# Moving a weight load, dummy products and a few rows of work in a fused two-block transformer kernel

## The chip, the cores and the metric

The kernel runs as one program on one core of one Trainium2 chip. The metric is the device time of one execution in microseconds (us). Before the change the median of 3 runs is 746.59 us (744.43 to 747.97).

## The reference

Two transformer blocks are computed on one sequence of 256 tokens with 1024 features, all in float32. The first block is an attention and pooling mixer followed by a mixture of 32 experts; the second is a hybrid mixer (attention and a recurrence) with a feed-forward layer.

```python
mod = jnp.matmul(c_act, w_ada[l]) + b_ada[l]
sh_m, sc_m, gt_m, sh_f, sc_f, gt_f = jnp.split(mod, N_MOD, axis=-1)
...
x = x + gt_m[:, None, :] * mix
h = modulate(rmsnorm(x, norm_ffn_g[l]), sh_f, sc_f)
ffn = hierarchical_moe(h.reshape(B * S, D), ...)
x = x + gt_f[:, None, :] * ffn.reshape(B, S, D)
...
for g in range(N_EXPERT_GROUPS):
    a = jnp.einsum('td,edf->tef', h, w_gate[g])
    b = jnp.einsum('td,edf->tef', h, w_up[g])
    act = jax.nn.silu(a) * b * comb[:, g, :, None]
    y = y + jnp.einsum('tef,efd->td', act, w_down[g])
...
xn = rmsnorm_2(x, norm1_g[layer])
u = xn @ w_in[layer].astype(f32)
```

`gt_f`, the gate row of the experts' output, is columns 5120 to 6143 of `mod`. The second block begins with the product of the normed result and its own `w_in`.

## The kernel before

**Pieces and their queue.** All large weights come from memory in 194 pieces of 1 MB (128 x 2048 float32), in the order of a list `pieces`: 36 for the first mixer, then the expert pieces from `E0` = 36 to `E1` - 1 = 131, then the second block's, whose first is piece `E1` (`w_in_2`). All are issued from SyncE (SP) by `sp_piece`, one after the other; `slot[i]` says into which of 25 places of SBUF piece i goes, and SP waits until the piece that was there before has been freed by the engine that read it. The list `ends` gives the places of the last 18 expert pieces. The places `HL` and `HL + 1` (raw15 and raw16 in the profile) share their memory with `XB`, the high and low parts of the normed input; `XP` is the memory of `X`, `XR` is `rawx`.

**Experts.** The 32 experts are worked off in 8 rounds y of 4 experts. A round has 8 pieces of gate and up weights (`pe_gate_up`, two halves of 4 pieces) and 4 pieces of down weights (`pe_down`, n = 0, 1 for the output half, f = 0, 1 for the piece). TensorE (PE) multiplies each piece in four strips of 32 rows (`psum<-raw,G` and `psum<-raw,XT`, 8 instructions a piece). Between them ScalarE (ACT) and VectorE (DVE) compute silu and product, PE turns the result (`pe_act`), DVE multiplies by the gate row (`dve_results`) and PE adds the result to the tokens in PSUM banks 4 to 7 (`pe_combine`, `psum<-ym,WT`). Ahead of round 7 every engine runs through the test of an overflow flag (a branch).

**Into the experts.** `dve_products` sums `w_ada` pieces weighted by `c` into `acc`; `pe_gate_row` then forms the gate row of half b by a product of ones with `acc`, plus a product with one row of ones for the bias `GTF`. In `pe_mixer`, `pe_mix_part`(n) is followed by `pe_back`(n - 1), which needs the DVE's row `x1`(n - 1) (L974). DVE works out the router (`dve_route`), up to the mask `MK`; PE ranks it (`psum<-MK,...`), DVE makes places and a selection `SS`, and PE gathers the tokens (`psum<-SS,XNH`). The first free place for the next expert piece comes when PE has multiplied the first one (`psum<-X,G`).

**Into the second block.** A piece of `w_in_2` is split by ACT into a high part (`whi`, L492) and by DVE into the rest (`wlo`, L503). `pe_n3` turns the experts' result, ACT and DVE make `XB` of it (`dve_n3`, L2163), and `feature_part` multiplies in groups of three matmuls (`psum<-XB,whi` twice, `psum<-XB,wlo` once).

**PSUM banks.** There are 8. `Banks(ids).take(e, name)` hands them out in the order of its list and lets the engine wait until the bank's last result has been read. The second block takes its banks from one such list nearly to its attention part, where `pe_z` has its own list `zb` = [0, 1, 2]. `pe_awake` is a dummy product, 128 x 512, whose result nobody reads.

Of the kernel before, what the change touches and what calls it, by code (L numbers as in the profile page):

```python
# [105 lines left out]
def build(nc, a, out):  # L106
# [3 lines left out]
    with root:  # L110
# [240 lines left out]
        for i in range(NP):  # L351
            if i == E0:
                last = homes[-NR - 1:]
                parts_ = [NR + k + NS * h for k in range(NS) for h in range(2)]
                turns = [XP] + last[0:5] + parts_[0:2] + last[5:] + parts_[2:] + [HL, HL + 1]
                first = turns[0:2] + [GP] + turns[2:12] + [YP] + turns[12:]
                ends = [NR, NR + NS] + parts_[2:6] + [(E1 + k) % NR for k in range(NR)] + parts_[6:] + [HL, HL + 1, XP]
            if pieces[i][0] == "exp":
                n = i - E0 - len(first)
                k = first[n] if n < 0 else turns[n % len(turns)] if i < E1 - len(ends) else ends[i - E1 + len(ends)]  # L360
                last_exp[k] = i
            elif i in fixed:
# [83 lines left out]
        def sp_load(e, upto):  # L446
            while cur["sp"] < min(upto, NP):
                i = cur["sp"]
                cur["sp"] += 1
                if i != E0:  # L450
                    sp_piece(e, i)
# [63 lines left out]
        def dve_products(e, b, k):  # L515
            s, i = acc[b % 2], ai[(b, k)]
            r = ring[slot[i]]
            e.wait_ge(*landed(i))
            for c in range(4):
# [84 lines left out]
        def pe_gate_row(e, banks, b):  # L604

            p = banks.take(e, ("ada", b))
            e.wait_ge(*loaded("gtf"))
            mm(e, p[:, :], ones[0:1, :], GTF[0:1, 512 * (b % 2):512 * (b % 2) + 512], True, False)
            e.wait_ge(*at(("acc", b)))
            mm(e, p[:, :], ones[:, :], acc[b % 2][:, :], False, True).then_inc(*moe_pe(("ada_sum", b), ("accread", b)))  # L610
# [56 lines left out]
        def feature_part(e, banks, j, cs, name, xname="n1", steps_=None):  # L667
            steps_ = steps_ or mix_pe
            h, l = whi[j % NS], wlo[j % NS]
            for q in range(2):  # L670
# [189 lines left out]
        def dve_mixer(e):  # L860
# [109 lines left out]
            dve_products(e, 11, 1)  # L970
            for n in range(8):
                e.wait_ge(*at(("mix_sum", n)))
# [317 lines left out]
        def pool_moe(e):  # L1290
            for n in X1:
                e.wait_ge(*at(n))
            overflow(e, "pool", None, None)
# [176 lines left out]
        def pe_moe(e, banks):  # L1470
# [3 lines left out]
            pe_awake(e, p, 2)  # L1474
# [11 lines left out]
            for y in range(NQ + 1):  # L1486
# [29 lines left out]
                if y < NQ:  # L1516
                    pe_gate_up(e, p, y, 1)
# [3 lines left out]
                if y and y != NQ - 1:  # L1521
                    for n in range(2):
                        pe_down(e, db, y - 1, n)
                        if y == NQ:
                            if n:
                                pe_n3(e, Banks([1]), 0)
                                pe_n3(e, Banks([3]), 1)
                            pe_combine(e, y - 1, n)
# [7 lines left out]
        def pe_down(e, db, y, n):  # L1536
            b = y % 2
            e.wait_ge(*at(("a", y)))
            p = db.take(e, ("d", y, n))
            for f in range(2):  # L1540
# [38 lines left out]
        def pe_gate_up(e, p, y, half):  # L1579
            g = y // 2  # L1580
            for c in range(4 * half, 4 * half + 4):
# [7 lines left out]
                x.then_inc(*moe_pe(("freed", i), *[("gu", y)] if c == 7 else []))  # L1589
            return p  # L1590
# [176 lines left out]
        def act_hybrid(e):  # L1767
            e.preload_act_table_set("natural_log_exp_and_others")
            for t in range(2):
                act_square(e, t, 0)  # L1770
            for q in range(4):
                if q == 2:
                    for t in range(2):
                        act_square(e, t, 1)
                high_part(e, E1 + q // 2, q % 2)
# [5 lines left out]
            act_pieces(e, E1 + 4)  # L1781
            for t in range(2):
# [169 lines left out]
        def dve_hybrid(e):  # L1952
# [3 lines left out]
            dve_results(e, NQ - 1, (1,))  # L1956
            low_part(e, E1, lo_dve, 0)
            dve_n3(e, 0)
            for t in range(2):
                dve_xg(e, t, 1)  # L1960
            low_part(e, E1, lo_dve, 1)
            dve_n3(e, 1)
            dve_n3(e, 2)
            low_part(e, E1 + 1, lo_dve, 0)
# [242 lines left out]
        def pe_hybrid(e, banks):  # L2207

            zb, ob, sb_, wb = Banks([0, 1, 2]), Banks([3, 4, 5, 6, 7]), Banks([2, 0, 1, 3]), Banks([4, 5, 6, 7])
            fb = Banks([0, 2])  # L2210
            feature_part(e, fb, w2(0), (0, 1), "f", "n3", hyb_pe)
            pe_n3(e, Banks([4]), 2)
            pe_n3(e, Banks([5]), 3)
            feature_part(e, fb, w2(0), (2, 3), "f", "n3", hyb_pe)
# [362 lines left out]
        def tensor_engine(e):  # L2577
            pe_mixer(e)
            pe_moe(e, Banks(list(range(8))))
            banks = Banks([6, 7, 0, 1, 2, 3, 4, 5])  # L2580
# [84 lines left out]
```

## Time and profile before

| | |
|---|---|
| median of 3 runs | 746.59 us |
| profiled execution, its own time | 746.17 us |
| span in its trace | 743.1 us |
| PE busy | 683.2 us (92%) |
| DVE busy | 390.0 us (52%) |
| ACT busy | 290.4 us (39%) |
| mean granted clock of TensorE | 0.963 |
| read from memory | 206.20 MB |

Times below are microseconds from the span's start. A granted clock of 1.00 is TensorE's full 2.4 GHz, 0.50 the lower level, 1.2 GHz. The chain that ended last is 67% PE and 19% DMA. A profile's "x" counts instructions; a float32 product is two of them.

### The profile page before, as it was taken

What the parts mean: (1) busy time and instruction counts of PE and PEld (TensorE: products, weight loads), DVE (VectorE), ACT (ScalarE), POOL (GpSimd) and SP (SyncE); (2) the same over time, 40 slices, a digit from 0 to 9 for tenths busy, and PEclk for the clock granted to TensorE, in tenths of its full rate; (3) what the DMA queues carried; (4) which work ended last, traced back from release to release, by engine and by line L of the source; (5) the groups of instructions that cost most, each with busy time, mean ns of one, the idle gap of its engine ahead of it and who ended that gap; (6) DMA issues with size and microseconds to landing.
All of it is one profiled execution on the core that took longest, in us unless ns stands there. A gap on an engine that the chain in (4) does not pass through costs nothing.

```text
span 743.1 us, 12343 instructions
## 1 busy us (share of the span) xinstructions
PE 683.2 (92%) x5124; PEld 514.0 (69%) x5124; DVE 390.0 (52%) x617; ACT 290.4 (39%) x425; POOL 53.9 (7%) x96
## 2 busy tenths in 40 slices
PE   4999998999978677777999999999999999999996
PEld 3897888653423121223999989998988888888885
DVE  3677776332110100104867987655876765665653
ACT  4245430241111010004676552578366544344532
POOL 0010000000000000000048650000000000000000
PEclk9999999799998798889999999999999999999998
DMA  9999999989999999999944534411654545664001
GB/s 369 426 423 417 387 392 415 427 343 424 427 427 426 426 427 427 424 426 427 365 191 160 209 120 161 171 58 62 228 210 158 217 144 206 227 227 168 3 1 56
DMA packets 29568, 208.10 MB, mean 280 GB/s; under 512 B 3266, under 2 KB 3522, under 8 KB 4676
## 3 DMA queue, kind: packets, MB, share of 16 engines
q1 hardware_dynamic: 29508, 207.26, 69.1%
q8 instruction: 43, 0.70, 0.4%
q14 instruction: 17, 0.14, 0.0%
HBM read 206.20 MB, written 1.05 MB: 279 GB/s over the span
## 4 chain that ended last, share of the span: by engine, by line
PE 67%; DMA 19%; DVE 6%; ACT 4%; issue 3%; SPq 1%; DVEq 0%; ACTq 0%
PE psum L429 65%; DMA raw<-in_w_exp 10%; DMA X<-in_w_exp 4%; DMA raw<-in_w_in 3%; DMA early<-in_w_ada_q 3%; PE psum L437 2%; DVE wlo L503 1%; DVE acc L525 1%; ACT whi L492 1%; ACT gates L1945 1%; SPq L468 0%; DVE X L2500 0%; ACT L1941 0%; DVE gates L2181 0%; DVE psum L2129 0%
## 5 line engine op out<-in xcount | busy, mean ns | idle before, releaser
L429 PE MATMUL psum<-XB,whi 128*128 128x256 f32 (+1 forms) x1216 | 267.1, 309 | 3.8 <-DVE XB L2163 1.6
L429 PEld LDWEIGHTS psum<-XB,whi 128*128 128x128 f32 x1216 | 197.4, 191 | 19.2 <-issue 3.9
L429 PE MATMUL psum<-XB,wlo 128*128 128x256 f32 x736 | 207.5, 282 | 0.0
L503 DVE TENSOR_TENSOR wlo<-raw,whi 128x2048 fp32r<-128x2048 f32 (+1 forms) x84 | 164.0, 1992 | 28.8 <-ACT whi L492 28.6
L492 ACT ACTIVATE whi<-raw 128x2048 fp32r<-128x2048 f32 (+1 forms) x77 | 135.3, 1798 | 47.4 <-PE psum L429 32.5
L429 PEld LDWEIGHTS psum<-XB,wlo 128*128 128x128 f32 x736 | 140.3, 191 | 0.2
L429 PE MATMUL psum<-raw,G 128*32 128x512 f32 x448 | 61.5, 666 | 20.1 <-DMA raw<-in_w_exp 11.7
L429 PEld LDWEIGHTS psum<-raw,G 128*32 128x32 f32 x448 | 14.0, 116 | 60.8 <-issue 31.5
L429 PE MATMUL psum<-whi,FH 128*128 128x512 f32 (+1 forms) x132 | 50.7, 384 | 0.0
L429 PE MATMUL psum<-whi,FL 128*128 128x512 f32 (+1 forms) x132 | 50.6, 384 | 0.0
L429 PE MATMUL psum<-wlo,FH 128*128 128x512 f32 (+1 forms) x132 | 50.6, 383 | 0.0
L1266 ACT ACTIVATE WT<-psum 128x256 f32<-128x256 f32 x8 | 3.1, 384 | 120.0 <-PE psum L429 83.8
L429 PE MATMUL psum<-whi,XB 128*128 128x512 f32 x128 | 42.4, 399 | 0.0
L1325 DVE TENSOR_TENSOR XT<-XT,psum 128x256 f32<-128x256 f32 x8 | 3.4, 422 | 73.6 <-ACT XT L1276 73.6
L429 PE MATMUL psum<-raw,XT 128*32 128x512 f32 x232 | 30.1, 638 | 8.5 <-DMA raw<-in_w_exp 7.2
L1337 DVE TENSOR_TENSOR ym<-psum,GT 128x512 f32<-128x512 f32 x16 | 11.1, 692 | 46.2 <-PE psum L429 46.2
L429 PE MATMUL psum<-ym,WT 128*128 128x512 f32 x64 | 33.8, 675 | 0.9 <-DVE ym L1337 0.9
L429 PEld LDWEIGHTS psum<-whi,FL 128*128 128x128 f32 x132 | 24.8, 188 | 5.0
L429 PEld LDWEIGHTS psum<-whi,FH 128*128 128x128 f32 x132 | 24.8, 188 | 5.0
L429 PEld LDWEIGHTS psum<-wlo,FH 128*128 128x128 f32 x132 | 24.8, 188 | 4.7
L429 PEld LDWEIGHTS psum<-whi,XB 128*128 128x128 f32 x128 | 24.0, 188 | 5.8 <-issue 0.4
L2464 DVE TENSOR_TENSOR af<-af,psum 128x512 f32<-128x512 f32 x16 | 11.0, 686 | 30.5 <-ACT af L2421 30.5
(374 smaller groups left out, 834.6 us busy)
## 6 DMA issues: line engine op xcount, KB each, us to landing
raw<-in_w_exp SPq DMA_DIRECT2D x85, 1024.0 KB, 25.5
raw<-in_w_ff SPq DMA_DIRECT2D x32, 1024.0 KB, 5.4
raw<-in_w_in SPq DMA_DIRECT2D x22, 1024.0 KB, 7.2
raw<-in_w_ada SPq DMA_DIRECT2D x15, 1024.0 KB, 10.6
raw<-in_w_in_t SPq DMA_DIRECT2D x8, 1024.0 KB, 19.4
X<-in_w_exp SPq DMA_DIRECT2D x5, 1024.0 KB, 26.0
rawx<-in_w_exp SPq DMA_DIRECT2D x4, 1024.0 KB, 16.7
raw<-in_w_out SPq DMA_DIRECT2D x4, 1024.0 KB, 5.3
```

What stands on the lines that cost most here:

```text
L429: return e.matmul(o, l, r, start=start, stop=stop, skip_group_check=True)
L437: return e.transpose(o, x, C["ident"][0:p, 0:p])
L492: e.activation(whi[j % NS][:, x], ring[slot[i]][:, x], ACT.Copy).then_inc(*hi_made(("hi", j), ("hi", j, x.start // 1024)))
L503: e.tensor_tensor(wlo[j % NS][:, x], ring[slot[i]][:, x], whi[j % NS][:, x], ALU.subtract).then_inc(*steps_(("lo", j, x.start // 1024), *[ ...
L525: x = e.scalar_tensor_tensor(out=s[:, :], in0=x, scalar=m, in1=s[:, :], op0=ALU.mult, op1=ALU.add)
L1266: e.activation(WT[y % 2][:, :], bank(("w", y))[:, 0:256], ACT.Copy).then_inc(*moe_act(("read", ("w", y)), ("WT", y)))
L1325: e.tensor_tensor(ac[b], sa[b], bank(("gu", y))[:, 256:512], ALU.mult).then_inc(*moe_dve(("read", ("gu", y)), ("act", y)))
L1337: e.tensor_tensor(ym[:, y % 2, cs], bank(("d", y, n))[:, :], GTF[:, cs], ALU.mult).then_inc(*moe_dve(("read", ("d", y, n)), ("y", y, n)))
L1945: e.activation(gates[:, n, :], gates[:, n, :], ACT.Sigmoid, bias=nbg[:, n:n + 1]).then_inc(*hyb_act(("sig", o)))
L2464: e.tensor_tensor(s, s, p[:, :, 0:256], ALU.add).then_inc(*ff_dve(*[("read", (("ff1", j), n)) for n in (2 * q, 2 * q + 1)]))
```

## The change

1. Piece `E1` is issued ahead of expert pieces `E1` - 2 and `E1` - 1, and `E1` - 2 lies in `rawx` instead of raw16, since `XB` is now written before that piece is used.
2. In round 7 a dummy product follows each of the last four gate and up pieces, each of the two pieces of the first down half, the first combine, and the first piece of the second down half: 8 in all. Combine and turns of the first output half come before the second down half. The second block's first products are cut into halves, and the last expert piece and the last combine stand between them.
3. ACT puts three of the four squares of the norm after its weight splits; DVE does both turns of the first half before the last result; the second block's banks come in the order 0, 1, 6, 7, 2, ... instead of 6, 7, 0, 1, 2, ....
4. The bias of the gate rows is added to `acc` by GpSimd (POOL), on one row; the two products with one row of ones are gone, and so are the two dummies ahead of the ranking.
5. DVE's last four products of `w_ada` are spread over the first rows of `x1`.

```diff
-                ends = [NR, NR + NS] + parts_[2:6] + [(E1 + k) % NR for k in range(NR)] + parts_[6:] + [HL, HL + 1, XP]
+                ends = [NR, NR + NS] + parts_[2:6] + [(E1 + k) % NR for k in range(NR)] + parts_[6:] + [HL, XR, XP]
...
-                if i != E0:
+                if i == E1 - 2:
+                    sp_piece(e, E1)
+                if i not in (E0, E1):
                     sp_piece(e, i)
...
             p = banks.take(e, ("ada", b))
-            e.wait_ge(*loaded("gtf"))
-            mm(e, p[:, :], ones[0:1, :], GTF[0:1, 512 * (b % 2):512 * (b % 2) + 512], True, False)
-            e.wait_ge(*at(("acc", b)))
-            mm(e, p[:, :], ones[:, :], acc[b % 2][:, :], False, True).then_inc(*moe_pe(("ada_sum", b), ("accread", b)))
+            e.wait_ge(*at(("biased", b)))
+            mm(e, p[:, :], ones[:, :], acc[b % 2][:, :], True, True).then_inc(*moe_pe(("ada_sum", b), ("accread", b)))
...
             dve_products(e, 11, 0)
-            dve_products(e, 11, 1)
             for n in range(8):
+                if n in (1, 2):
+                    dve_products(e, 11, 1, range(2 * n - 2, 2 * n))
...
         def pool_moe(e):
+            e.wait_ge(*loaded("gtf"))
+            for b in (10, 11):
+                e.wait_ge(*at(("acc", b)))
+                e.tensor_tensor(acc[b % 2][0:1, :], acc[b % 2][0:1, :], GTF[0:1, 512 * (b % 2):512 * (b % 2) + 512], ALU.add).then_inc(
+                    *mix_pool(("biased", b)))
...
             p = Banks([3]).take(e, "rank")
-            pe_awake(e, p, 2)
...
-                    pe_gate_up(e, p, y, 1)
+                    pe_gate_up(e, p, y, 1, y == NQ - 1)
...
+            y = NQ - 1
+            for f in range(2):
+                pe_down(e, db, y, 0, (f,))
+                pe_awake(e, ps[0], 1)
+            pe_combine(e, y, 0)
+            pe_awake(e, ps[0], 1)
+            pe_n3(e, Banks([1]), 0)
+            pe_n3(e, Banks([3]), 1)
+            pe_down(e, db, y, 1, (0,))
+            pe_awake(e, ps[2], 1)
...
                 x.then_inc(*moe_pe(("freed", i), *[("gu", y)] if c == 7 else []))
+                if awake:
+                    pe_awake(e, ps[0], 1)
...
-            fb = Banks([0, 2])
-            feature_part(e, fb, w2(0), (0, 1), "f", "n3", hyb_pe)
-            pe_n3(e, Banks([4]), 2)
-            pe_n3(e, Banks([5]), 3)
-            feature_part(e, fb, w2(0), (2, 3), "f", "n3", hyb_pe)
+            fb = Banks([2, 4])
+            feature_part(e, fb, w2(0), (0, 1), "f", "n3", hyb_pe, (0,))
+            pe_down(e, None, NQ - 1, 1, (1,))
+            e.wait_ge(*at(("sq", 0, 0)))
+            holder.pop(4)
+            feature_part(e, fb, w2(0), (0, 1), "f", "n3", hyb_pe, (1,))
+            pe_combine(e, NQ - 1, 1)
+            feature_part(e, fb, w2(0), (2, 3), "f", "n3", hyb_pe, (0,))
+            pe_n3(e, Banks([1]), 2)
+            pe_n3(e, Banks([3]), 3)
+            feature_part(e, fb, w2(0), (2, 3), "f", "n3", hyb_pe, (1,))
...
-            banks = Banks([6, 7, 0, 1, 2, 3, 4, 5])
+            banks = Banks([0, 1, 6, 7, 2, 3, 4, 5])
```

On SP, at the end of the expert pieces, the queue read before (`raw`, `X` and `rawx` are places, `in_w_exp` the experts' weights, `in_w_in` the second block's first weight):

```order
L468 DMA raw<-in_w_exp 128x2048 x11
L468 DMA X<-in_w_exp 128x2048
L468 DMA raw<-in_w_in 128x2048 x14
```

and it reads now:

```order
L470 DMA raw<-in_w_exp 128x2048 x10
L470 DMA raw<-in_w_in 128x2048
L470 DMA rawx<-in_w_exp 128x2048
L470 DMA X<-in_w_exp 128x2048
L470 DMA raw<-in_w_in 128x2048 x13
```

One `in_w_in` piece has gone ahead of the last two expert pieces, and the first of those two goes to `rawx`.

On PE, between the last router logits (`psum<-GT,XT`) and the gather (`psum<-SS,XNH`), before:

```order
L429 MATMUL psum<-GT,XT 128x36 x8
L429 MATMUL psum<-GT,ones 128x512
L429 MATMUL psum<-acc,ones 128x512
L429 MATMUL psum<-GT,ones 128x512
L429 MATMUL psum<-acc,ones 128x512
L429 MATMUL psum<-cst 128x512 x2
L429 MATMUL psum<-MK,cst 128x32
L429 MATMUL psum<-MK,ones 128x32
```

and now:

```order
L429 MATMUL psum<-GT,XT 128x36 x8
L429 MATMUL psum<-acc,ones 128x512 x2
L429 MATMUL psum<-MK,cst 128x32
L429 MATMUL psum<-MK,ones 128x32
```

Two one-row products (`psum<-GT,ones`) and two dummies (`psum<-cst`) are gone; the dummy behind the ranking, ahead of the gather, stays.

On PE in round 7, from the last four gate and up pieces on, the difference is:

```order
 L429 MATMUL psum<-ym,WT 128x512 x4
-L429 MATMUL psum<-raw,G 32x512 x16
+L429 MATMUL psum<-raw,G 32x512 x4
+L429 MATMUL psum<-cst 128x512
+L429 MATMUL psum<-raw,G 32x512 x4
+L429 MATMUL psum<-cst 128x512
+L429 MATMUL psum<-raw,G 32x512 x4
+L429 MATMUL psum<-cst 128x512
+L429 MATMUL psum<-raw,G 32x512 x4
+L429 MATMUL psum<-cst 128x512
 L437 MATMUL psum<-cst,XT 128x128 x2
```

Every piece's product is now followed by a dummy of 128 x 512.

## Rows read from the trace of the kernel before

**Rows 1.** Windows of 1 us: length, busy time by engine, granted clock, DMA share, GB/s
```profile
138.00:139.00 1.00, 1.00 (x3) 0.04 (x1) 0.96 (x7) 1.00 (x2) 0.00 (x0) 0.50 1.02 434
...
151.00:152.00 1.00, 1.00 (x11) 1.00 (x10) 1.00 (x2) 0.24 (x1) 0.00 (x0) 1.00 0.75 315
152.00:153.00 1.00, 0.75 (x10) 0.58 (x12) 0.70 (x5) 1.00 (x3) 0.00 (x0) 1.00 0.23 98
153.00:154.00 1.00, 1.00 (x12) 0.39 (x15) 0.14 (x1) 0.98 (x4) 0.00 (x0) 1.00 0.12 49
154.00:155.00 1.00, 1.00 (x12) 0.31 (x8) 0.83 (x7) 1.00 (x1) 0.00 (x0) 1.00 0.08 33
155.00:156.00 1.00, 1.00 (x16) 0.32 (x8) 0.88 (x5) 0.13 (x1) 0.00 (x0) 1.00 1.05 164
156.00:157.00 1.00, 1.00 (x12) 0.51 (x5) 1.00 (x4) 0.00 (x0) 0.00 (x0) 1.00 0.90 360
```

**Rows 2.** The chain that ended last, in order of time: start, us, what
```profile
321.60 24.05 DMA raw<-in_w_in
...
348.94 3.12 PE psum L429 x24
...
352.93 73.01 PE psum L429 x726
```

**Rows 3.** PE's timeline into the experts: start, us, what, idle before
```profile
121.53 0.71 PE L429 MATMUL psum<-cst,XT 128*128 128x128 f32 x4 [1.87 <-DVE XT L974]
...
137.39 1.64 PE L429 MATMUL psum<-GT,ones 1*128 1x512 f32 x2
138.96 2.07 PE L429 MATMUL psum<-acc,ones 128*128 128x512 f32 x2
...
144.83 3.51 PE L429 MATMUL psum<-cst 128*128 128x512 f32 x4
...
150.54 0.47 PE L429 MATMUL psum<-SS,XNH 128*128 128x256 f32 x2 [0.22 <-DVE r L1412]
```

**Rows 4.** DVE's timeline into the experts
```profile
115.53 5.55 DVE L525 SCALAR_TENSOR_TENSOR acc<-raw,cact,acc 128x512 f32<-128x512 f32 x7
...
141.44 0.23 DVE L1391 TENSOR_TENSOR MK<-MK,r 128x64 f32<-128x64 f32 x1
...
149.42 0.22 DVE L1394 SCALAR_TENSOR_TENSOR MK<-psum,MK 128x64 f32<-128x64 f32 x1 [6.43 <-PE psum L429]
```

**Rows 5.** SP's issue of the next expert piece
```profile
154.04 0.33 SPq L468 DMA_DIRECT2D X<-in_w_exp  x1
```

**Rows 6.** PE's timeline, round 7 and the second block's start
```profile
326.41 3.60 PE L429 MATMUL psum<-ym,WT 128*128 128x512 f32 x8
329.94 2.78 PE L429 MATMUL psum<-raw,G 128*32 128x512 f32 x24
333.37 1.06 PE L429 MATMUL psum<-raw,G 128*32 128x512 f32 x8 [0.65 <-DMA raw<-in_w_exp]
...
336.41 3.36 PE L429 MATMUL psum<-raw,XT 128*32 128x512 f32 x16 [0.52 <-DVE XT L1314]
340.69 1.96 PE L429 MATMUL psum<-ym,WT 128*128 128x512 f32 x4 [0.92 <-DVE ym L1337]
...
348.94 0.47 PE L429 MATMUL psum<-XB,whi 128*128 128x256 f32 x2 [1.59 <-DVE XB L2163]
```

**Rows 7.** Window of PE's down products in round 7
```profile
337.00:338.00 1.00, 1.00 (x8) 0.00 (x0) 0.00 (x0) 0.00 (x0) 0.00 (x0) 0.50 1.09 459
```

**Rows 8.** PE at the first attention scores (z)
```profile
465.05 0.93 PE L429 MATMUL psum<-GT 64*128 64x256 f32 x8
```

**Rows 9.** The same stretch on DVE
```profile
463.59 0.69 DVE L2181 TENSOR_TENSOR gates<-psum,rqrow 128x512 f32<-128x512 f32 x1 [0.35 <-PE psum L429]
466.41 0.61 DVE L2041 TENSOR_SCALAR hon<-psum,hrs 128x128 f32<-128x128 f32 x2 [2.13 <-ACT hrs L1938]
```

**Rows 10.** What PE waited for from 350 to 743
```profile
PE psum L429 <- DVE psum L2129: 0.9, 1, 0.9
```

More of the change, by code:

```diff
@@ L513, in dve_pieces, with dve_products @@
                     low_part(e, i, lo_dve)
-        def dve_products(e, b, k):
+        def dve_products(e, b, k, cs=range(4)):
             s, i = acc[b % 2], ai[(b, k)]
             r = ring[slot[i]]
-            e.wait_ge(*landed(i))
-            for c in range(4):
+            if cs[0] == 0:
+                e.wait_ge(*landed(i))
+            for c in cs:
                 x, m = r[:, 512 * c:512 * c + 512], cact[:, 4 * k + c:4 * k + c + 1]
@@ L664, in act_high, with feature_part @@
                 e.activation(XH[:, sl, :], XT[:, sl, :], ACT.Copy).then_inc(*steps_((name, "H", q)))
-        def feature_part(e, banks, j, cs, name, xname="n1", steps_=None):
+        def feature_part(e, banks, j, cs, name, xname="n1", steps_=None, qs=range(2)):
             steps_ = steps_ or mix_pe
             h, l = whi[j % NS], wlo[j % NS]
-            for q in range(2):
+            for q in qs:
                 p = bank((name, q)) if cs[0] else banks.take(e, (name, q))
@@ L1520, in pe_moe @@
                             pe_gather(e, gb, y // 2 + 1, 2 * (y % 2) + q)
-                if y and y != NQ - 1:
+                if y and y < NQ - 1:
                     for n in range(2):
                         pe_down(e, db, y - 1, n)
[L1524 to L1528, printed above, removed]
+            y = NQ - 1
[8 more added lines that the diff above has]
+            pe_awake(e, ps[2], 1)
         def pe_act(e, tb, y):
@@ L1534, in pe_act, with pe_down @@
             turn(e, p[:, 128:256], ac[y % 2][:, 128:256]).then_inc(*moe_pe(("act_turned", y)))
-        def pe_down(e, db, y, n):
+        def pe_down(e, db, y, n, fs=range(2)):
             b = y % 2
             e.wait_ge(*at(("a", y)))
-            p = db.take(e, ("d", y, n))
-            for f in range(2):
+            p = bank(("d", y, n)) if fs[0] else db.take(e, ("d", y, n))
+            for f in fs:
                 i = xi[(y, 8 + 2 * n + f)]
@@ L1577, in pe_gather, with pe_gate_up @@
             i.then_inc(*moe_pe(("gathered", g, q)))
-        def pe_gate_up(e, p, y, half):
+        def pe_gate_up(e, p, y, half, awake=False):
             g = y // 2
@@ L1768, in act_hybrid @@
             e.preload_act_table_set("natural_log_exp_and_others")
-            for t in range(2):
-                act_square(e, t, 0)
             for q in range(4):
                 if q == 2:
-                    for t in range(2):
-                        act_square(e, t, 1)
-                high_part(e, E1 + q // 2, q % 2)
+                    act_square(e, 0, 0)
+                if q % 2 == 0:
+                    for part in range(2):
+                        high_part(e, E1 + q // 2, part)
                 e.wait_ge(*at(("n3", "turned", q)))
@@ L1781, in act_hybrid @@
             act_pieces(e, E1 + 4)
+            for t, n in ((1, 0), (0, 1), (1, 1)):
+                act_square(e, t, n)
             for t in range(2):
@@ L1955, in dve_hybrid @@
                 dve_xg(e, t, 0)
-            dve_results(e, NQ - 1, (1,))
             low_part(e, E1, lo_dve, 0)
             dve_n3(e, 0)
+            dve_n3(e, 1)
+            low_part(e, E1, lo_dve, 1)
+            dve_results(e, NQ - 1, (1,))
             for t in range(2):
                 dve_xg(e, t, 1)
-            low_part(e, E1, lo_dve, 1)
-            dve_n3(e, 1)
+            low_part(e, E1 + 1, lo_dve, 0)
             dve_n3(e, 2)
-            low_part(e, E1 + 1, lo_dve, 0)
             dve_n3(e, 3)
```

## The prediction

> **What bounds the kernel now.** I read the slices of the span first, then the chain that ended last, then the timelines around the places that the change touches. Up to about 346 us the DMA engines are full: the chain's last long DMA is the second block's first piece, issued at 321.60 and landed 24.05 later, at 345.67 [rows 2]. One gap is in that stream: in the windows from 151 to 157 the rate falls from 426 GB/s to 315, 98, 49, 33, 164 and 360 [rows 1]. The missing bytes are (111 + 328 + 377 + 393 + 262 + 66) / 426 = 3.6 us of full rate. The next expert piece was issued at 154.04 [rows 5], long after the ones before it, since its place is free only when PE has multiplied the first expert piece, behind the gather at 150.54 [rows 3]. So the router's length sets when the stream goes on, and whatever the gap loses is lost at 345.67 too. From 348.94 on PE is the bound: the chain has 73.01 us of PE in one stretch from 352.93 [rows 2], and later PE's longest wait for DVE is 0.9 us [rows 10].
>
> **Part A, into the experts (items 4 and 5).** PE waits 1.87 us at 121.53 for the first `x1` row [rows 3], which stands behind eight DVE products of 5.55 / 7 = 0.79 each [rows 4]. With four of them put behind it, the row is there about 3 us sooner, and PE finds it waiting: 1.87 gained. The two pairs moved behind rows 0 and 1 take 1.6 us each, beside 1.9 us of PE work per row, so they fit. The POOL additions have from about 123 to 135 for two one-row operations; I cost them at nothing; if that cover were gone, the second gate row would wait for them.
>
> Then PE: the one-row products take about 1.6 and 2.0 us (137.39 to 138.96, and as much as a full product for the second), the two dummies 3.51 [rows 3]. They stand ahead of the ranking, whose mask is ready at 141.44 + 0.23 = 141.67 [rows 4], while the ranking comes at 148.3 and DVE waits 6.43 us for it until 149.42 [rows 4]. Without them the gate rows start at 137.39 - 1.87 = 135.5 and end at 137.6 to 139.6, by the clock; the mask comes at 139.8 and is what ranking waits for next. Ranking takes 1.2 us, DVE meanwhile has 1.4 us of low rows, so places are made at about 141.3 instead of 149.42, and the first piece is freed some 8 us sooner: SP issues at about 146, not 154.04. At the lower clock throughout (ranking 2.4, a dummy 1.75 [rows 3], gather and product doubled) it is 149.5. The stream runs dry at 151.2 and a piece needs about 2 us from issue to full rate (154.04 to the window from 156, [rows 1, 5]), so 149.2 is the latest issue that closes the gap. Term A is therefore -3.6 us, with -3.3 at the slow end. The rest of the 8 us is worth nothing: PE meets its next DMA wait sooner.
>
> The clock matters here. It fell to 0.50 in the window from 138 with PE busy 1.00 [rows 1], ahead of it the 36-column router products and the one-row product; being busy alone did not hold it. The Trainium skill (TensorE: Matmul & The Clock Gate, Part 1) says that activity releases the throttle and idleness brings it back, so by it a busy PE would keep the full clock here; the trace differs. By the page the issue would be at 146, by the row up to 149.5, and term A -3.6 or -3.3.
>
> **Part B, round 7 and the turn to the second block (items 1 to 3).** All times here are in the old frame, 3.6 less in the new. By the order on SP, `in_w_in` lands two pieces sooner, 2 x 1.048576 MB / 426 GB/s = 4.9 us, at 340.8, and the last expert piece at 345.67 instead. Moving it past costs the queue no starvation, for what SP issues at 321.60 lands 24 us later. What PE then does, at 0.86 for a piece at full clock (three in 329.94 to 332.5), 0.88 for a dummy or a combine product (3.53 / 4), 0.36 for a group of three `XB` products (24 products in 3.12 less the last one's tail, 2.96 [rows 2]), so 1.44 for four:
>
> The last four gate and up products start at 329.94. With dummies, c5, c6, c7 start 1.74 apart, c7 at 335.16 instead of 333.37, where it waited for its piece: 1.79 later. Its own dummy lies in the wait for silu. The down products start at 336.41 + 1.79 = 338.20. They took 3.36 for two because the granted clock was 0.50 [rows 6, 7]; at full clock they take 1.72, plus one dummy, and end 1.03 later than now (340.80). The dummy behind them covers the 0.92 wait for DVE. Combine at 341.72, to 343.60; dummy to 344.48; turns 0.79, to 345.27; first piece of the second half to 346.13; dummy to 347.01; first half group of `XB` to 348.45 (XB is ready at 346.6); last expert piece, landed at 345.67, to 349.31; second half group 350.75; combine 352.63; then 1.44, turns 0.79, and 7.20 of the first weight's and the next one's products: 362.06. Before, the same point was 348.94 + 2.96 + 0.79 + 8.64 = 361.33. Term B is +0.7 us. So DMA no longer is what this stretch waits for; PE itself is, with about 7 us of dummies of which roughly half lie in old waits.
>
> Its bounds. If PE were there when the last piece lands, what is left behind it is 0.86 + 1.44 + 1.88 + 1.44 + 0.79 + 7.20 = 13.6, to 359.3: -2.0. If PE fell to the lower clock among the dummies in spite of them, eight dummies and eight pieces would cost another 0.87 each for as long as it lasts; half of them is +7, which I take as the far end.
>
> Item 3, the squares: ACT's three later squares come at about 360 to 362, PE's factor row comes 5.8 us into `q2`, at about 367.9; ACT and DVE need some 3 us behind the squares, so it is covered; without this cover it costs about 1 us.
>
> **Part C, the bank order (the last line of the diff).** The hybrid's bank list is turned. Counting takes: q2, g2, i2, sq 8; heads, sk, sv, values and turns make 32 up to `on` 2; the 33rd is gate (4, 0) and the 34th the values of head 3. Before, those were banks 6 and 7, and `pe_z` 0 and 1 right behind them took banks 0 and 1, read long ago. Now they are banks 0 and 1. So z 0 waits for DVE's read of gate (4, 0), over at 463.59 + 0.69 = 464.28, ahead of z at 465.05: nothing. But z 1, which started at 465.05 + 0.45 = 465.5, waits for the read of head 3's values, which DVE starts only at 466.41, when ACT has made the norm's factor of them (DVE waited 2.13 us for it), and ends at 467.02 [rows 8, 9]. That is a new stall of 1.5 us. Queued behind it on PE is the whole second half of gate 4, and PE is the bound there (waits of 0.9 us at most [rows 10]), and what ACT waits for next (a weight place that this gate frees) moves with it. Term C is +1.5; bounds 0 (if the later waits swallow it) and +1.9.
>
> **The sum.** Against the profiled execution's 746.17 us (span 743.1 and 3.07 around it): -3.6 + 0.7 + 1.5 = -1.4, to 744.8. That execution is 0.42 below the median of 746.59, so I forecast 745.2 us.
>
> **The rivals.**
> 1. The tail pays as well: PE is there when the last piece lands, B is -2.0. For it speaks that the piece lands 2.8 us before I have PE at it, so any slack in my PE times would be turned into gain; against it the dummies, counted from rows. 746.6 - 3.6 - 2.0 + 1.5 = 742.5.
> 2. The new bank wait costs nothing, because ACT and DVE, not PE, set the pace behind 472. 746.6 - 3.6 + 0.7 = 743.7. Against it: the ACT steps there are themselves released by this gate.
> 3. The change does not do what it says into the experts: the gap stays, since the first place is freed at about the old time (gate rows held up by the POOL additions, or by anything that brings issue to 154). Then only the costs remain: 746.6 + 0.7 + 1.5 = 748.8, slower than before, by 0.3%. It decides when issue is later than about 153. Against it are 8 us of removed PE work in a stretch where DVE waited 6.43 us for PE.
> 4. The clock stays low in round 7 and the dummies run at 1.75 instead of 0.88: up to +7, about 751. For it: PE comes out of the branch at the lower clock. Against it: from 326.41 on combine products took 0.88, so the full clock is back there, and PE is now busy without a pause until 336. The Trainium skill (the same page, Part 1) agrees that sustained products bring the full clock, and by it this case has no place.
>
> **How the numbers follow.** Forecast (A, B, C as costed) 0.52; rival 1 0.17; rival 2 0.15; rival 3 0.08; rival 4 0.05; 0.03 for both 1 and 2 together, 741.0. The time is that of the forecast, 745.2. The range runs from 742.0, just under rival 1, to 748.4, short of rival 3; outside it are rival 4, most of rival 3 and the combination of 1 and 2. The likeliest case alone has 743.7 to 746.7. What a measurement of this kernel can tell from no change is about 0.5%, 3.7 us: faster means under 742.9, slower over 750.3. Rival 1, the two together and a part of rival 2's spread are faster: 0.24. Rival 4 is slower: 0.05. The same: 0.71.
>
> **What would show it.** In the changed profile: no wait of PE ahead of `pe_back` 0; places at about 141 instead of 149.42; issue of the next expert piece at 146 to 149.5, and no window under 400 GB/s from 151 to 157; the first `w_in_2` piece landed near 337, the last expert piece near 342, and PE at it some 3 us later; granted clock 1.00 from the combine of round 6 on; the factor row's product, 16 groups into `q2`, at 362.06 - 3.6 + 5.8 = 364.3 instead of 361.33 + 5.8 = 367.1; and a PE wait of about 1.5 us behind ACT and DVE at the first scores, near 462. The prediction is wrong if the gap stays, if the router leaves the clock low into the gather for longer than assumed, or if PE's products in round 7 run at another clock than 1.00.

## The result, and the profile after

The changed kernel takes 749.30 us (median of 7 runs, 748.84 to 750.68) against 745.85 us (7 runs, 744.17 to 747.97) of the kernel before: ratio 1.0051, 95% interval 1.0030 to 1.0072. It is slower, by 3.8 us by the ratio and 3.5 between the two medians, where 745.2 was forecast with a range up to 748.4. The profiled execution took 748.84 us, its span is 747.0.

**Into the experts.** PE's timeline after, which answers to [rows 3]:

```profile
135.05 1.96 PE L429 MATMUL psum<-acc,ones 128*128 128x512 f32 x4
139.57 0.38 PE L429 MATMUL psum<-MK,cst 128*128 128x32 f32 x2 [2.56 <-DVE MK L1398]
...
142.00 0.77 PE L429 MATMUL psum<-SS,XNH 128*128 128x256 f32 x2
```

DVE's and SP's timelines at the same place, which answer to [rows 4, 5]:

```profile
140.88 0.23 DVE L1401 SCALAR_TENSOR_TENSOR MK<-psum,MK 128x64 f32<-128x64 f32 x1
```

```profile
146.38 0.33 SPq L470 DMA_DIRECT2D X<-in_w_exp  x1
```

And windows of 1 us, in the columns of [rows 1]:

```profile
143.00:144.00 1.00, 1.00 (x6) 1.00 (x6) 0.97 (x5) 0.00 (x0) 0.00 (x0) 0.50 0.97 410
...
154.00:155.00 1.00, 1.00 (x12) 0.20 (x2) 0.00 (x0) 0.07 (x1) 0.00 (x0) 1.00 1.03 434
```

Both gate rows take 1.96 us together, PE now waits for the mask and not the mask for PE, places are made at 140.88 instead of 149.42, SP issues at 146.38 instead of 154.04, and the gap in the stream is gone: 434 GB/s in the window that had 33.

**Round 7 and the turn.** PE's timeline, which answers to [rows 6]:

```profile
317.32 6.02 PE L429 MATMUL psum<-raw,G 128*32 128x512 f32 x32 [6.03 <-issue]
...
327.08 1.07 PE L429 MATMUL psum<-raw,G 128*32 128x512 f32 x8
328.07 1.12 PE L429 MATMUL psum<-cst 128*128 128x512 f32 x2
329.13 1.06 PE L429 MATMUL psum<-raw,G 128*32 128x512 f32 x8
...
336.28 1.06 PE L429 MATMUL psum<-raw,XT 128*32 128x512 f32 x8 [0.52 <-DVE XT L1321]
...
340.30 1.95 PE L429 MATMUL psum<-ym,WT 128*128 128x512 f32 x4
...
345.47 0.80 PE L429 MATMUL psum<-XB,whi 128*128 128x256 f32 x2
...
347.40 1.07 PE L429 MATMUL psum<-X,XT 128*32 128x512 f32 x8
...
349.93 1.88 PE L429 MATMUL psum<-ym,WT 128*128 128x512 f32 x4
...
367.14 0.61 PE L429 MATMUL psum<-hon,ones 128*128 128x128 f32 x4
```

PE is ahead by 2.3 us when round 7 starts (317.32, before 319.61) and has lost it all at the factor row (367.14, before 367.17). It hardly waits here: nearly every old wait is filled, with more than it held. The clock is 1.00 from 323 on, as forecast. The first `w_in_2` piece landed at 338.71 and the last expert piece at 343.5 (forecast near 337 and 342); PE came to the latter 3.9 us behind its landing, at 347.40, where some 3 us were forecast.

**At the first scores.** The same view, which answers to [rows 8]:

```profile
465.61 0.92 PE L429 MATMUL psum<-GT 64*128 64x256 f32 x4
467.64 0.92 PE L429 MATMUL psum<-GT 64*128 64x256 f32 x4 [1.11 <-DVE hon L2055]
```

and a window behind it:

```profile
469.00:470.00 1.00, 1.00 (x7) 1.00 (x7) 0.44 (x2) 0.94 (x3) 0.00 (x0) 0.50 0.00 0
```

z 1 waits as forecast, but the two z take 2.88 us instead of 0.86, and behind the wait the granted clock is 0.50 until 472 (before it was 1.00 throughout). The chain that ended last has DVE and ACT in it where [rows 2] has 73.01 us of PE:

```profile
382.92 2.30 DVE wlo L505
385.36 41.16 PE psum L429 x458
...
458.37 7.36 PE psum L429 x70
467.64 8.37 PE psum L429 x52
```

The shift against the kernel before, in us from the span's start: -2.3 at round 7, 0.0 at the factor row, +0.6 at z 0, +4.0 at the 248 products in one stretch (514.40, now 518.42), +3.9 at the end.

### The profile page after: what moved, and what is told of

It is laid out like the page before. It is cut to its first block, busy times and chain, and to the rows that moved or that the text cites. A ratio compares the mean times of both kernels' runs of the same rounds, so it can differ in the third digit from the quotient of the medians.

```text
span 747.0 us, 12366 instructions
## 1 busy us (share of the span) xinstructions
PE 686.0 (92%) x5132; PEld 514.0 (69%) x5132; DVE 390.5 (52%) x617; ACT 289.9 (39%) x425; POOL 56.0 (7%) x98
## 4 chain that ended last, share of the span: by engine, by line
PE 65%; DMA 19%; ACT 6%; DVE 6%; issue 3%; SPq 1%; DVEq 0%; ACTq 0%
PE psum L429 63%; DMA raw<-in_w_exp 12%; DMA X<-in_w_exp 3%; DMA early<-in_w_ada_q 3%; DVE wlo L505 2%; PE psum L437 2%; ACT whi L494 2%; ACT gates L1959 1%; SPq L470 0%; DVE X L2520 0%; DVE XT L1321 0%; ACT L1955 0%; DVE gates L2195 0%; ACT gates L1797 0%; DVE psum L2143 0%
## 5 line engine op out<-in xcount | busy, mean ns | idle before, releaser
L429 PE MATMUL psum<-raw,G 128*32 128x512 f32 x448 | 64.3, 687 | 17.3 <-DMA raw<-in_w_exp 9.2
L429 PE MATMUL psum<-ym,WT 128*128 128x512 f32 x64 | 31.0, 628 | 0.0
L429 PEld LDWEIGHTS psum<-raw,XT 128*32 128x32 f32 x224 | 5.9, 110 | 33.1 <-DMA raw<-in_w_exp 14.3
```

What stands on the lines that cost most here:

```text
L429: return e.matmul(o, l, r, start=start, stop=stop, skip_group_check=True)
```

## The experiments

Each line of this table is a kernel: its median, the ratio to the kernel before on the same chip, and from its one profiled execution the span and four places on PE: the first product of round 7, the factor row, z 0, and the stretch of 248 products. The kernel before had medians of 743.9 to 745.0 beside them.

| kernel | us | ratio (95%) | span | round 7 | factor | z 0 | x248 |
|---|---|---|---|---|---|---|---|
| before | 745.85 | | 743.1 | 319.61 | 367.17 | 465.05 | 514.40 |
| after | 749.30 | 1.0051 (1.0030-1.0072) | 747.0 | 317.32 | 367.14 | 465.61 | 518.42 |
| r_router | 743.06 | 0.9970 (0.9953-0.9987) | 740.6 | 317.31 | 364.39 | 462.27 | 511.61 |
| a_banks67 | 745.92 | 1.0020 (1.0002-1.0038) | 743.9 | 317.63 | 367.11 | 465.60 | 514.93 |
| a_nodummy | 746.55 | 1.0022 (1.0000-1.0044) | 744.5 | 318.51 | 364.45 | 462.93 | 515.76 |
| b_banks01 | 748.04 | 1.0039 (1.0016-1.0062) | 746.8 | 321.28 | 368.57 | 466.44 | 517.79 |
| c_clean | 743.27 | 0.9979 (0.9961-0.9998) | 739.9 | 317.05 | 363.07 | 461.53 | 510.85 |
| c_e1back | 747.76 | 1.0044 (1.0026-1.0062) | 744.0 | 317.40 | 367.54 | 466.00 | 515.31 |
| a_down4 | 747.35 | 1.0032 (1.0013-1.0052) | 744.6 | 317.64 | 364.26 | 462.73 | 515.54 |
| r_two | 742.41 | 0.9963 (0.9947-0.9980) | 740.6 | 318.00 | 364.37 | 462.25 | 511.56 |
| c_squares | 742.09 | 0.9966 (0.9947-0.9985) | 740.5 | 318.59 | 364.61 | 462.49 | 511.82 |
| a_zdummy | 747.96 | 1.0037 (1.0017-1.0056) | 745.8 | 317.85 | 367.42 | 465.88 | 517.20 |
| b_norank | 744.70 | 0.9999 (0.9981-1.0017) | 743.2 | 320.29 | 367.31 | 465.19 | 514.50 |
| b_spread | 742.78 | 0.9974 (0.9956-0.9991) | 740.2 | 317.47 | 363.98 | 461.86 | 511.18 |
| b_item4 | 742.90 | 0.9980 (0.9965-0.9995) | 742.2 | 318.63 | 365.92 | 463.81 | 513.12 |
| b_bias | 743.11 | 0.9976 (0.9963-0.9989) | 741.9 | 318.17 | 366.08 | 463.96 | 513.28 |

Executions of one kernel scatter by 2 to 7 us from the fastest to the slowest, so I read differences between two places of one trace, which scatter less, and use medians and ratios for the sign. There is one trace of each kernel.

### The router part alone: r_router

The kernel before, with items 4 and 5 of the change and nothing else.

> The kernel before with items 4 and 5 alone (bias of the gate rows on POOL, no dummies ahead of the ranking, the last products spread over the x1 rows). My theory, term A: the gap of 3.6 us in the DMA stream at 151 to 157 closes, the first w_in_2 piece lands 3.6 us sooner, at about 342.1, and the end comes about 3 us sooner, since PE, which waits for that piece's XB in this part of the program, also has its own idle of 5.6 to 6 us ahead of round 7 that does not shrink: -2.5 to -3.6 us against the kernel before. Rival: PE's own chain, not the stream, sets the turn to the second block, and what the gap gives back is absorbed there: 0 to -1.5 us.

Measured -2.2 us by the ratio (interval -3.5 to -1.0), -2.8 at the factor row. The gap is closed. But PE's own chain takes a part back (0.7 us, by r_two below), in PE's timeline:

```profile
334.79 1.87 PE L429 MATMUL psum<-raw,XT 128*32 128x512 f32 x8 [0.74 <-DMA raw<-in_w_exp]
337.55 3.75 PE L429 MATMUL psum<-ym,WT 128*128 128x512 f32 x4 [0.88 <-DVE ym L1342]
```

The combine takes 3.75 instead of 1.96 at the clock of 0.50 that follows the small waits. Term A's mechanism holds; its size is inside what was expected by the trace and a little under it by the ratio.

### The bank order: a_banks67, b_banks01, a_zdummy

```diff
             feature_major(e, banks, w2(8), "n3", hyb_pe, "sq")
+            banks.ids = [6, 7, 0, 1, 2, 3, 4, 5]    # a_banks67, in the changed kernel
+            banks.ids = [0, 1, 6, 7, 2, 3, 4, 5]    # b_banks01, in the kernel before
```

> The changed kernel with the bank list turned back to 6, 7, 0, 1, ... behind the fourth column product (sq), so that z 0 and z 1 take banks read long ago. In the changed kernel's trace z 1 waits and the two z take 2.9 us instead of 0.86; right behind it the granted clock is 0.50 from 469 to 472, which costs another 1.5 us. Theory 1: both go with the bank wait, -3.5 us against the changed kernel (about 745.8), and no window under 1.00 at 466 to 476. Theory 2: the clock falls there for another reason, only the stall goes, -2.0 us (747.3). Theory 3: the later waits give the wait back, -1 or less.

> The kernel before with only the bank order of the changed kernel, set behind the fourth column product (sq), so that the 33rd and 34th takes are banks 0 and 1 there too. Theory 1 (stall of z 1 of 2.0 us and 1.5 us of products at the low clock behind it): +3.5 us against the kernel before, PE's wait for hon at about 467 and windows of 0.50 behind it. Theory 2 (my prediction's term C): +1.5. Theory 3: the loss behind 458 in the changed kernel has to do with other parts of the change: 0.

From z 0 to the 248 products it takes 49.35 us before, 52.81 after, 49.33 in a_banks67, 51.35 in b_banks01. So the order alone costs 2.0 us, and the other 1.5 of the 3.46 come with the clock: in b_banks01 the same wait was followed by full clock, in PE's timeline and a window:

```profile
466.44 0.92 PE L429 MATMUL psum<-GT 64*128 64x256 f32 x4
468.47 0.92 PE L429 MATMUL psum<-GT 64*128 64x256 f32 x4 [1.11 <-DVE hon L2041]
```

```profile
470.00:471.00 1.00, 1.00 (x11) 1.00 (x10) 0.56 (x1) 0.97 (x3) 0.00 (x0) 1.00 0.00 0
```

By the ratios a_banks67 is 2.3 us under the changed kernel and b_banks01 2.9 us over the kernel before (interval 1.2 to 4.6). That settles the sign, and not whether the wait costs 2.0 or 3.5 us in the usual execution.

To test that the fall comes of the idle time, a dummy was put into the wait:

```diff
                                 pe_z(e, zb, 0)
+                                e.wait_ge(*at(("read", holder[2])))
+                                pe_awake(e, ps[2], 1)
                                 pe_z(e, zb, 1)
```

> The changed kernel with one dummy product (bank 2) between z 0 and z 1, where PE waits some 1.1 us for hon. In three of four traces with this wait the granted clock fell to 0.50 for about 3 us right behind it (in the changed kernel at 469 to 472) and in one it did not. Theory 1: the fall comes from the idle time; with the dummy no window of 0.50 at 466 to 474 and -1.5 us against the changed kernel by the trace, with the stall itself (2.0 us) still there. Theory 2: the fall has nothing to do with the idle time: it stays in most runs, and the time too.

PE's timeline of it:

```profile
465.88 0.92 PE L429 MATMUL psum<-GT 64*128 64x256 f32 x4
466.73 1.13 PE L429 MATMUL psum<-cst 128*128 128x512 f32 x2
467.91 0.92 PE L429 MATMUL psum<-GT 64*128 64x256 f32 x4
```

No window from 462 to 476 is under 1.00, and z 0 to the 248 products takes 51.32 us: the stall of 2.0 is there and the 1.5 of the clock is not. The fall came in three of the four traces with the bare wait (after, a_nodummy, a_down4) and in none of the 11 without a wait at that place, so the wait brings it. That a dummy in the wait prevents it fits theory 1, but rests on this one trace, and b_banks01 had no fall without a dummy; the median against the changed kernel (ratio 1.0037 against 1.0051) has the sign, but not the resolution.

### The dummies: a_nodummy, a_down4

a_nodummy takes out all eight calls of `pe_awake` in and behind round 7; a_down4 only the first four:

```diff
-                    pe_gate_up(e, p, y, 1, y == NQ - 1)
+                    pe_gate_up(e, p, y, 1)
```

> The changed kernel without its eight dummy products in round 7 and behind it. In its trace PE runs without a pause from 327.1 to 343 and reaches the last expert piece 5 us behind its landing; a piece with a dummy takes 2.05 us there, 0.99 without. Theory 1: the dummies are what ate the gain of the router, since only about half of each lies in an old wait; without them the factor row's product comes 2 to 3.5 us sooner than 367.14 and the end too (746 to 747). Theory 2: without dummies the waits of some 1 us let the granted clock fall to 0.50, as at 337 in the kernel before, and the products at that clock cost what the dummies did: within 0.7 us of the changed kernel.

> The changed kernel without the four dummies behind the gate and up pieces of round 7; the four in the down half and behind it stay. By the trace without any dummies, the turn behind silu stands at 333.26 with c4 at 328.26 (5.00), with them at 335.35 with c4 at 327.08 (8.27): these four should cost 3.3 us and the other four nearly nothing, so about -2.5 to -3.3 us against the changed kernel. Rival: the loss is spread evenly over the eight: -1.4.

From the start of round 7 to the factor row it takes 49.82 us after, 45.94 in a_nodummy, 46.62 in a_down4. So all eight cost 3.9 us there, of which the four behind the gate and up pieces are 3.2. PE's timeline of a_nodummy shows the old waits open again and the clock at 1.00 in spite of them, in this trace:

```profile
328.26 3.94 PE L429 MATMUL psum<-raw,G 128*32 128x512 f32 x32
333.26 0.41 PE L437 MATMUL psum<-cst,XT 128*128 128x128 f32 x2 [1.05 <-DVE XT L1332]
...
338.04 1.96 PE L429 MATMUL psum<-ym,WT 128*128 128x512 f32 x4 [0.89 <-DVE ym L1344]
```

By the traces it is theory 1 for both. By the ratios a_nodummy is 2.2 us under the changed kernel and a_down4 1.4, which is what its rival had; the intervals are too wide to choose by them.

The low clock that the dummies were to prevent came at the down products of round 7 in only 4 of the 11 traces that have no dummy around there (before, r_router, c_e1back, b_bias).

### What is left of the new turn: c_clean, c_e1back, c_squares

c_clean joins a_nodummy and a_banks67.

> The changed kernel without its eight dummies and with the bank list turned back behind the fourth column product: the router part and the new order at the turn alone. If the two repairs add up (2.7 us at the factor row by the trace without dummies, 3.5 us behind 458 by the trace with the old banks), its span is 747.0 - 2.7 - 3.5 = 740.8, within 0.5 us of the span of the kernel before with the router part alone (740.6): then the new order at the turn, with w_in_2 ahead, is worth nothing. Rival: the two overlap, since a PE that comes sooner to z waits longer there: 742 or more.

The repairs add up: 739.9. Its ratio (0.9979) is not told apart from r_router's (0.9970). From round 7 to the factor row it takes 46.02 us against 47.08, so the new turn gains 1.1 us there over r_router (0.5 over b_spread's 46.51, where the clock had not fallen), and 0.6 of it is lost again up to z 0 (98.46 us, before 97.88).

c_e1back is c_clean without the move of piece `E1`:

```diff
-                if i == E1 - 2:
-                    sp_piece(e, E1)
-                if i not in (E0, E1):
+                if i != E0:
```

> The kernel c_clean with the first w_in_2 piece issued behind the last two expert pieces again; PE's order stays the new one. This prices item 1 inside the new order. The piece then lands 4.9 us later, at about 342, ACT and DVE need some 2.5 us to split it, and PE, which was at its first XB product at 343.1 without dummies, would be there at about 344.5 to 346: +1.5 to +3 us against c_clean. Rival: the last expert piece, which then lands sooner, gives as much back: 0.

+4.5 us by the medians, more than the 3 expected, and 50.14 us from round 7 to the factor row. In PE's timeline the second half waits for its input:

```profile
343.33 1.06 PE L429 MATMUL psum<-rawx,XT 128*32 128x512 f32 x8
346.19 0.47 PE L429 MATMUL psum<-XB,whi 128*128 128x256 f32 x2 [1.80 <-DVE XB L2172]
```

Part of it is a combine of 3.75 us at the low clock, as in r_router. So PE's new order needs item 1, but the two together hardly beat the old order.

c_squares is c_clean with this edit in `act_hybrid`:

```diff
+                if q == 2:
+                    for t, n in ((1, 0), (0, 1), (1, 1)):
+                        act_square(e, t, n)
                 e.wait_ge(*at(("n3", "turned", q)))
...
-            for t, n in ((1, 0), (0, 1), (1, 1)):
-                act_square(e, t, n)
```

> The kernel c_clean with ACT's three later squares moved up, ahead of its wait for the third turn (ACT idled 3.2 us there, from 346.4 to 349.7). It takes 0.58 us more from the factor row's product to the anchor in front of the first scores (91.21 us) than the old order (90.63), with a PE wait of 0.4 us for DVE's wlo at about 381. Theory 1: that is the price of item 3, since the squares behind the splits delay the factors, DVE's chain and the next splits by 0.7 us: the wait goes, and the end comes 0.4 to 0.6 us sooner (span 739.3 to 739.5), which the median will hardly show, but the trace will. Theory 2: the 0.58 us comes from DVE's order, not from the squares: nothing changes.

Factor row to z 0 takes 97.88 us, as before the change, and the chain that ended last is PE's again, where that of after had ACT and DVE:

```profile
351.60 71.79 PE psum L429 x714
```

Theory 1 by this stretch; the span (740.5) did not become shorter, since round 7 began 1.5 us later in this trace, and the median (742.09) can't show 0.6 us.

### Two dummies, in two waits: r_two

```diff
                     pe_gate_up(e, p, y, 1)
+                    if y == NQ - 1:
+                        pe_awake(e, ps[0], 1)
...
                         pe_down(e, db, y - 1, n)
                         if y == NQ:
+                            if n == 0:
+                                pe_awake(e, ps[0], 1)
```

> The kernel before with the router part (items 4 and 5) and two dummies only, each in a wait: one behind the last gate and up piece of round 7 (PE waited 1.05 us for silu there) and one behind the second down piece (0.88 us for DVE). In the run with the router part alone the granted clock was 0.50 from 335 to 341 and the down products and the combine there took 1.87 and 3.75 instead of 1.06 and 1.96, 2.6 us more. Theory 1: the dummies keep the clock and cost 0.2 us beyond their waits: -1 to -2.5 us against the router part alone (span 738 to 739.6), to where the landing of w_in_2 at about 342 binds. Theory 2: what PE gains there it waits for XB, since that is made from the piece and from the first combine: 0 to -0.8. Theory 3: the clock falls anyway: +0.5.

The clock stayed at 1.00 and the last combine started 1.9 us sooner than in r_router (342.43 against 344.30), but `XB`'s first product began at 346.14 (346.17 without them). Round 7 had begun 0.7 us later here, so the two dummies are worth 0.7 us: 46.37 us from there to the factor row, against 47.08. Theory 2: `w_in_2` landed at 342.87 and binds. b_spread has 46.51 with no dummy, since the clock had not fallen there.

### Which part of the router carries it: b_spread, b_norank, b_item4, b_bias

The kernel before with item 5 alone (b_spread), without the two dummies ahead of the ranking (b_norank), with all of item 4 (b_item4), with the bias on POOL alone (b_bias).

> The kernel before with item 5 alone: the last four w_ada products behind the first rows of x1. PE's wait of 1.87 us at 121.5 goes and everything up to the ranking comes 1.9 us sooner, so that the next expert piece is issued at 152.2 instead of 154.04. Theory 1: the gap shrinks by 1.9 us, to 1.7, and the end comes 1 to 1.9 us sooner. Theory 2: the acc row for the second gate row is late now and takes the gain away again: 0.

> The kernel before without the two dummies ahead of the ranking, nothing else. They took 3.51 us at the low clock, and the ranking waited for them, not for the mask. The next expert piece is then issued 3.5 us sooner, at 150.5, 1.3 behind the latest issue that I worked out for a closed gap (149.2). Theory 1: some 2.3 of the 3.6 us come back: w_in_2 lands 2.3 us sooner and the end comes 1.5 to 2.3 us sooner. Theory 2: the gap closes in full and the one-row products and the DVE order buy nothing: as the router part alone, -2.5 to -3. Theory 3: the clock, without the dummies, is low in the gather, and the issue comes at 152: -1.

> The kernel before with item 4 alone (bias rows on POOL, no one-row products, no dummies ahead of the ranking), DVE's order as before. PE still waits 1.87 us at 121.5. Theory 1 (my working): gate rows end at 141.5 at the latest, ranking follows the mask (141.7), places at 143.2, issue at about 148.5: the gap closes and the end comes as with the whole router part, -2.5 to -3.5 us. Theory 2: the wait at 121.5 lets the granted clock fall at 122 to 125 in part of the executions, which moves everything by 1.4 us; the gap still closes (issue by 150), but the front is later, -1.5 to -2.5. Theory 3: without the dummies the clock is low in the gather, and the issue comes behind 151: 0 to -1, as with the dummies alone removed.

> The kernel before with the bias rows on POOL alone; the two dummies ahead of the ranking stay. The one-row products took 1.6 and 2.0 us at the low clock, 3.6 in all, so ranking comes up to 3.6 us sooner and the issue at 150.4. Theory 1: most of the gap closes, -1.5 to -3 us. Theory 2: as with the dummies alone, nothing, since one wait at the low clock takes the place of the other.

SP's issue of the next expert piece, in b_spread, b_norank and b_item4:

```profile
150.18 0.33 SPq L468 DMA_DIRECT2D X<-in_w_exp  x1
```

```profile
154.41 0.33 SPq L468 DMA_DIRECT2D X<-in_w_exp  x1
```

```profile
152.66 0.33 SPq L468 DMA_DIRECT2D X<-in_w_exp  x1
```

In b_bias it came at 149.90. For b_item4 theories 2 and 3 both came: the clock fell behind the wait, and it was low in the gather, with the issue behind 151; by the ratio it is -1.5 us. For b_bias it is theory 1 (-1.8). Three of the four are faster (0.9974, 0.9980, 0.9976) and b_norank is not (0.9999). Item 5 alone closes the gap but for one window (377 GB/s at 152). Its 1.87 us became 3.86, for the clock was low from 137 to 144 there, before from 137 to 148. In b_norank the clock fell behind the wait of 1.87 us, and again at 139 with the one-row products, and then stayed low until 152, through ranking and gather, where before it was back at 148; in windows of 1 us:

```profile
124.00:125.00 1.00, 1.00 (x7) 1.00 (x6) 0.48 (x1) 0.00 (x0) 0.00 (x0) 0.50 1.03 434
150.00:151.00 1.00, 1.00 (x6) 1.00 (x5) 1.00 (x2) 0.00 (x0) 0.00 (x0) 0.50 1.01 426
```

The dummies had spent 3.5 us, but without them the gather ran at half speed: theory 3. Issue came later than theory 3 had it (154.41, not 152), and the fall at 122 has 1.4 us of that. Whether it is so in every execution, one trace doesn't tell; the median, which shows no gain, fits it. The wait at 121.5 was followed by the low clock in three of the five traces that have it (b_banks01, b_norank, b_item4; not in before and b_bias), which moves all PE work behind it by 1.4 to 1.6 us; no trace with item 5 has the wait.

In b_bias and b_item4 that wait grew to 2.8 us. The cause is in the durations of DVE's products there (least, median and largest in ns, in b_bias):

```profile
L526 DVE SCALAR_TENSOR_TENSOR acc<-raw,cact,acc x8: 752/753/1661, 114.3 to 121.3; 128x512 f32<-128x512 f32 x8
```

The one of 1661 ns runs beside POOL's addition (115.22, 1.49 us). The changed kernel has the same (1666 ns), hidden by item 5.

## Why the prediction was wrong

**Term A, -3.6: right in its mechanism, somewhat large.** Every sign named for it came: no wait ahead of `pe_back` 0, places at 140.88, issue at 146.38, no window under 400. At the factor row the router part alone is worth -2.8 (r_router) to -3.2 (b_spread), in the median -2.2. Two steps under it were off. The POOL additions were costed at nothing and take 0.9 us from DVE. And the 8 us of removed PE work were far more than was needed: item 5 alone gives the term, as far as these runs can tell. Where I held that the clock could fall with PE busy, the traces sort themselves: the four with the one-row products (before, b_banks01, b_norank, b_spread) fall at 137 to 139 with PE busy; in the twelve without them it holds until PE has waited for the mask (2.6 us, 0.75 in b_bias), to 140 at least. The 36-column products stand ahead of that place in all 16, so they alone don't bring it.

**Term B, +0.7: this is the first step that failed; it measured +2.8.** The factor row was forecast at 364.3 and stands at 367.14, 2.8 us late: 0.8 of it is what term A fell short by, about 2 are B's. Against the forecast times PE is late by 0.74 at the fifth piece (326.34 forecast, 327.08), 1.68 at the down products (334.60, 336.28), 2.18 at the combine (338.12, 340.30), 2.55 at the last expert piece (344.85, 347.40) and 2.78 at the last combine (347.15, 349.93). The first 0.74 is A's gain, which I carried over in full: PE came to its idle time ahead of round 7 2.75 us sooner, not 3.6, and that idle time does not shrink (5.57, now 6.03). The rest is what it costs PE to go from the strips (128*32 in the rows) to full products (128*128) and back, at the dummies and at the last expert piece between the `XB` groups. "0.86 for a piece at full clock, 0.88 for a dummy" was read from rows in which like follows like; in turn they take 0.99 and 1.06, 2.05 for a pair instead of 1.74. The Trainium skill (TensorEngine Tiling (Array Packing), Key Properties) says that a change of tiling mode drains TensorE. By it each change between strips and full products costs something: the trace agrees, with 0.31 us a pair.

A second reading in B was wrong too: what the first four dummies buy. From the fifth piece to the first down product it was 6.47 us before, 8.26 were forecast with them, and it takes 9.20; in a_nodummy 5.93. So they cost 3.3 us there, not 1.79, for the wait for the last of these pieces, 0.65 before, was shorter where they had been laid; only the one behind that piece lies wholly in a wait. In return I booked 1.64 us for down products at full clock, taken from the trace before; in a_nodummy and c_clean the clock was full there without them. B's bound of -2.0 was not reached even without dummies: c_clean's factor row is 4.1 us sooner than before, 1.3 beyond r_router's 2.8.

**Item 3, costed at nothing: 0.6 us** (c_squares), which I had named as about 1 if the cover was gone. It was gone at another place, at DVE's `wlo` (PE waits 0.35 for it at 381.30 in c_clean).

**Term C, +1.5: right in place and cause, too small by 2.0; this is the second step that failed.** A quarter of the miss is the z pair. I let z 1 start 0.45 behind z 0 and charged the stall from there, as if each took half of the pair. The row behind [rows 8], before:

```profile
465.91 0.51 PE L429 MATMUL psum<-XB,whi 128*128 128x256 f32 x2
```

Two z in a row take 0.86 together and each takes 0.85 alone, since they use different halves of the 128 rows (64*128 in the rows): parting them loses their overlap, and the stall costs 2.0. The Trainium skill (TensorEngine Tiling (Array Packing), Key Properties) says that different tiles can load weights and multiply in parallel, and the trace agrees. The other 1.5 is the clock, which I had not connected with a wait of 1.1 us: met in three of four traces with the wait, in none of 11 without it, and absent in the one trace with a dummy in it.

**The sum.** By the runs: A -2.8, dummies and turn +2.8, squares +0.6, z +2.0 and clock +1.5 make +4.1; the spans differ by 3.9, the medians by 3.5. The bank order and the dummies alone turn a gain into a loss; none of my rivals had both. Rival 3 names 748.8, close to what was measured, but by a gap that stays open; the gap closed, so that its number comes near is chance.

## What to carry to other kernels

A dummy product pays only in a wait that will still be there once everything ahead of it has moved; price it by a row in which it alternates with the work around it. When a bank or buffer list is turned, look up who holds each bank where it is taken next, and whether the two products that the wait parts ran side by side; a wait of 1 us can cost 3.5. And try the parts of a change singly: one reordering on DVE gave as much (0.9974) as can be told apart here: the best versions (r_two at 0.9963, c_squares at 0.9966) lie within its interval.

## What was not expected of the hardware

- A wait of PE of 1.1 us was followed by 3 us at the clock of 0.50 in three of four traces, one of 1.87 to 2.8 us in three of five. Whether it falls differs between executions of the same instructions, and costs PE 1.4 to 1.6 us each time.
- While products with one row of ones ran, the clock fell to 0.50 with PE busy, in four traces of four; without them it was full at the same place (b_bias: PE busy at 1.00 until it waits at 142).
- A DVE product of 128 x 512 with two operands in SBUF took 1661 ns instead of 753 beside a POOL addition of a single row. The Trainium skill (GPSIMD Engine Reference, Specifications) says that GpSimd shares its SBUF interfaces with VectorE, with contention when a DVE instruction has two SBUF inputs; the trace agrees.
- Before round 7 PE idles 5.3 to 6.0 us in every trace for nothing that the profile names, whenever it arrives; no run here touched it.
